# Opening block merged into the first products' block, transfers in order of use, zero products at the opening

## The chip, the cores and the metric

The kernel runs on one core of one Trainium2 chip. The metric is the device time in microseconds, as the median of several runs. The profile and the trace are of one execution on the chip; their times are microseconds from the span's start.

## The reference, cut to what matters

Two transformer-like layers over T = 512 tokens of width 1024. The change touches only the start of the first one: a root-mean-square norm and the first matrix product.

```python
h = rmsnorm(x, norm_mix[i])
u = h @ w_in[i]
u_rwkv = u[..., :RWKV_COLS]
u_da = u[..., RWKV_COLS:RWKV_COLS + DA_COLS]
```

`rmsnorm` divides each token by the root of its mean square and multiplies by the gain `norm_mix`. Since the divisor belongs to a token, the kernel applies it behind the product.

## The kernel before

Everything is kept transposed, channels on the 128 partitions and the 512 tokens along the row; x is 8 tiles (index k) of 128x512. A **job** is one output tile: a weight tile of 128x1024 (8 blocks of 128x128) times the 8 tiles of h. For precision each operand is cut into a high half (`w_hi`, `h_hi`, rounded to fp32r) and a low half (`w_lo`, `h_lo`), so a job is 8 times the three matmuls of lines 367 to 369, 24 in all, of 512 columns each.

The program is a row of blocks with a barrier between them. In the first, the **opening block** (line 2873), SyncE issues the loads (`params`, weight tiles 0 and 1, x in four transfers of two tiles each, `consts`, weight tiles 2 and 3, `w_lora`), and VectorE derives four small constants from `params` (lines 2888 to 2894). The second is `gemm_block` (line 306) with the stages `DaIn` (12 jobs) and `Shift` (15 jobs).

`gemm_block` writes out each engine's order by hand. SyncE streams weight tiles into four raw slots; a tile waits until the low half of the tile four before it is made. ScalarE makes `w_hi` (line 390) and VectorE `w_lo` (line 408), into three slots. The function `due` says how early: before the stage's own work of job g they take all tiles up to the job's own plus the look-ahead, which is `first_ahead` = 1 for job 0 and `AHEAD` = 2 afterwards, as far as a slot is free. TensorE goes through batches of jobs; `DaIn` puts jobs 0 and 1 in one batch and alternates between them at each k. Ahead of a batch, a loop over its jobs issues the waits for their `w_lo`.

In `DaIn`, at job 0, ScalarE makes for each k `h_hi` (line 755) and the square of x (line 760, into the two-row buffer `norm_sq`), VectorE makes `h_lo` (line 765), and GpSimd adds the squares into `norm_pair` (line 778; six adds). ScalarE then loads a table of functions. Ahead of job 2 TensorE sums the squares over partitions by two products with ones (`NormSum.pe`, lines 785 and 787), and at job 1 in ScalarE's order `NormSum.finish` makes `norm_rstd` by a log (line 792), a table load and an exp (line 797). VectorE's outputs (line 658) of jobs 0, 1 and 2 all stand at job 2 in its order, the first behind a wait for `norm_rstd`. From job 3 on attention work (`DiffAttention`, `beside`) is woven in: rotations on TensorE (line 491), their tables loaded by GpSimd's queue behind the square-sum (lines 456 and 457), and sums on VectorE (lines 589 to 593).

Of the kernel before, what the change touches and what calls it, by code (L numbers as in the profile page):

```python
# [16 lines left out]
F32 = mybir.dt.float32  # L17
# [154 lines left out]
BANKS = 4  # L172

# [97 lines left out]
class Stage:  # L271
# [7 lines left out]

    def before(self, pe, n):  # L280
        pass
# [24 lines left out]
def gemm_block(pr, hi, lo, stages, first_ahead=AHEAD, pe_after=nothing, act_after=nothing, dve_after=nothing, sp_after=nothing,  # L306
               sp_between=nothing, behind=nothing):
# [20 lines left out]
    def due(split, g):  # L328

        if split >= tiles or split > weight(g) - first_tile + (AHEAD if g else first_ahead):  # L330
            return False
        s = pr.split_no[first_tile + split] - 1
        return s < SPLIT_SLOTS or pr.last_job[pr.split_slot[s - SPLIT_SLOTS]] <= first + g

    with nc.Block() as block:
# [10 lines left out]
        def _(pe):  # L346
            for batch in batches:
# [10 lines left out]
                for k in range(kt):  # L358
                    for g in batch:
                        stage, n = order[g]  # L360
                        stage.ready(pe, n, k)
                        job = stage.jobs[n]
                        slot = (pr.split_no[job.weight] - 1) % SPLIT_SLOTS
                        w_hi, w_lo = hi[:, slot, k * P:(k + 1) * P], lo[:, slot, k * P:(k + 1) * P]
                        x_hi, x_lo = job.moving[k]
                        out = bank(g)[:, 0:job.width]
                        nc.tensor.matmul(out, w_hi, x_hi, start=(k == 0), stop=False)  # L367
                        nc.tensor.matmul(out, w_hi, x_lo, start=False, stop=False)  # L368
                        last = nc.tensor.matmul(out, w_lo, x_hi, start=False, stop=(k == kt - 1))  # L369
                        if k == kt - 1:  # L370
                            last.then_inc(pr.job_done, 1)
# [8 lines left out]
        def _(act):  # L380
            split = 0
# [15 lines left out]
        def _(dve):  # L397
            split = 0
# [222 lines left out]
class DaIn(Stage):  # L621
# [54 lines left out]
    def pool(self, pool):  # L676
        self.norm.pool(pool)
# [64 lines left out]
class NormSum:  # L742
# [19 lines left out]
    def dve(self, dve, k):  # L762
        if self.gain is not None:
# [3 lines left out]
                .then_inc(self.pr.sum_lo, 1)  # L767

# [2066 lines left out]
def bass_two_blocks(nc, dram, out):  # L2835

    with ExitStack() as ctx:
# [30 lines left out]
        with ExitStack() as in_scope:  # L2868
            hi = pr.tile("w_hi", [P, SPLIT_SLOTS, 1024], F32R, in_scope)
            lo = pr.tile("w_lo", [P, SPLIT_SLOTS, 1024], F32R, in_scope)  # L2870
            loaded, consts_in, made, lora_in = (pr.sem(k) for k in ("params_in", "consts_in", "derived_made", "lora_in"))
            x_in = [pr.sem(f"x_in{j}") for j in range(KT // 2)]
            with nc.Block() as block:
                @block.sync
                def _(sp):
                    sp.dma_start(params[:, :], dram["params"]).then_inc(loaded, 16)
                    pr.stream(sp, 2)
                    for k in range(0, KT, 2):
                        sp.dma_start(x[:, k:k + 2, :], x_view(dram["x"])[:, k:k + 2, :]).then_inc(x_in[k // 2], 16)
# [4 lines left out]
                @block.vector  # L2884
                def _(dve):
                    dve.wait_ge(loaded, 16)

                    nc.vector.tensor_tensor(derived[:, 0:15], pr.param_cols("mu_prev"), pr.param_cols("mu_next"),
                                            ALU.add).then_inc(made, 1)
                    dve.wait_ge(made, 1)  # L2890
                    nc.vector.tensor_scalar(derived[:, 0:15], derived[:, 0:15], -1.0, 1.0, ALU.mult, ALU.add).then_inc(made, 1)
                    nc.vector.tensor_scalar(derived[:, 15:19], pr.param_cols("k_a"), -1.0, 1.0, ALU.mult, ALU.add)\
# [210 lines left out]
```

## Time and profile before

| | |
|---|---|
| median of 3 runs | 1804.69 us (1802.5 to 1805.23) |
| span of the profiled execution | 1802.6 us; no other time of this execution is given |
| TensorE matmuls | 1718.9 us busy, 95% |
| VectorE | 1050.2 us, 58% |
| ScalarE | 705.3 us, 39% |
| GpSimd | 112.8 us, 6% |
| HBM traffic | 94 GB/s over the span |

Busy shares are averages over the whole span. A matmul's duration contains its drain, so the pace is read from the distance between starts. "Idle before" in a row is the time in which the engine stood, with who released it.

### The profile page before, as it was taken

The page shows a single profiled execution, that of the slowest core. Times are in us where ns is not written, and L with a number is a line of the kernel's source. Part 1 is how long each engine was busy: PE and PEld are TensorE (multiplying, and loading weights), DVE is VectorE, ACT ScalarE, POOL GpSimd, SP SyncE. Part 2 cuts the span into 40 slices and gives each one's busy share as a digit, 9 for nine tenths or more (in the row PEclk, how much of TensorE's full clock was granted, in tenths as well). Part 3 has the DMA queues.
Part 4 walks back from the last instruction along what each step waited for, and adds up shares of the span by engine and source line. Part 5 has one row for each costly group of instructions (what it writes and reads, how often), then busy time and mean ns, then how long its engine had stood idle before and what let it go on. Part 6 is the DMA issues. An engine that isn't in the chain of part 4 may idle for free. (4 is left out here: it accounts for less than half of the span.)

```text
span 1802.6 us, 29740 instructions
## 1 busy us (share of the span) xinstructions
PE 1718.9 (95%) x12674; PEld 1350.5 (75%) x12674; DVE 1050.2 (58%) x1461; ACT 705.3 (39%) x1051; POOL 112.8 (6%) x132
## 2 busy tenths in 40 slices
PE   7999999999999999999999889998898899999997
PEld 5666768888876888888888678874476678888885
DVE  6757586667537657677665763117785544343433
ACT  4344544424236443232314443235664433142322
POOL 2000000000000100001111100003100100000001
PEclk9999999999999999999999999999999999999998
DMA  5212221011044344446562222230001222322321
GB/s 201 67 59 77 93 85 38 32 43 38 20 162 161 117 164 140 170 141 226 192 212 84 73 82 71 82 118 2 1 1 48 82 82 94 105 94 94 105 94 47
DMA packets 49076, 171.16 MB, mean 95 GB/s; under 512 B 5536, under 2 KB 6944, under 8 KB 48176
## 3 DMA queue, kind: packets, MB, share of 16 engines
q1 hardware_dynamic: 39184, 133.00, 21.6%
q0 software_dynamic: 9760, 36.25, 6.0%
q8 instruction: 101, 1.65, 0.4%
q14 instruction: 31, 0.25, 0.0%
HBM read 160.84 MB, written 8.39 MB: 94 GB/s over the span
## 5 line engine op out<-in xcount | busy, mean ns | idle before, releaser
L367 PE MATMUL pair<-h_hi,w_hi 128*128 128x512 f32 x1032 | 417.6, 405 | 33.1 <-DVE w_lo L408 15.5
L369 PE MATMUL pair<-h_hi,w_lo 128*128 128x512 f32 x1032 | 405.6, 393 | 0.0
L368 PE MATMUL pair<-h_lo,w_hi 128*128 128x512 f32 x1032 | 405.5, 393 | 0.0
L408 DVE TENSOR_TENSOR w_lo<-w_raw,w_hi 128x1024 fp32r<-128x1024 f32 (+2 forms) x225 | 265.8, 1183 | 201.2 <-ACT w_hi L390 201.1
L390 ACT CAST w_hi<-w_raw 128x1024 fp32r<-128x1024 f32 (+2 forms) x225 | 221.9, 989 | 225.3 <-PE pair L369 221.2
L367 PEld LDWEIGHTS pair<-h_hi,w_hi 128*128 128x128 f32 x1032 | 196.2, 190 | 92.3 <-DVE w_lo L408 31.6
L368 PEld LDWEIGHTS pair<-h_lo,w_hi 128*128 128x128 f32 x1032 | 196.3, 190 | 42.7 <-issue 3.8
L369 PEld LDWEIGHTS pair<-h_hi,w_lo 128*128 128x128 f32 x1032 | 195.8, 190 | 41.9
L367 PE MATMUL pair<-ff_f_hi,w_hi 128*128 128x512 f32 x512 | 199.7, 390 | 0.6 <-issue 0.6
L369 PE MATMUL pair<-ff_f_hi,w_lo 128*128 128x512 f32 x512 | 199.2, 389 | 0.0
L368 PE MATMUL pair<-ff_f_lo,w_hi 128*128 128x512 f32 x512 | 199.2, 389 | 0.0
L2480 ACT ACTIVATE ff_sq<-ff_relu 128x512 f32<-128x512 f32 x64 | 40.5, 632 | 219.6 <-DVE ff_relu L2509 110.4
L367 PEld LDWEIGHTS pair<-ff_f_hi,w_hi 128*128 128x128 f32 x512 | 96.1, 188 | 20.8 <-issue 1.0
L369 PEld LDWEIGHTS pair<-ff_f_hi,w_lo 128*128 128x128 f32 x512 | 96.1, 188 | 19.9
L368 PEld LDWEIGHTS pair<-ff_f_lo,w_hi 128*128 128x128 f32 x512 | 96.1, 188 | 19.9
L2512 DVE TENSOR_TENSOR ff_f_lo<-ff_sq,ff_f_hi 128x512 fp32r<-128x512 f32 x64 | 44.3, 693 | 86.5 <-ACT ff_f_hi L2484 86.5
L2520 DVE SCALAR_TENSOR_TENSOR x<-pair,mod,x 128x512 f32<-128x512 f32 x32 | 24.0, 751 | 88.9 <-PE pair L369 88.9
L2381 DVE SCALAR_TENSOR_TENSOR mod_acc<-mod_w,silu_c,mod_acc 128x1024 f32<-128x1024 f32 x56 | 71.4, 1279 | 1.2 <-DMA mod_w<-in_w_mod 0.9
L861 PE MATMUL pair<-h_hi,gate_hi 128*128 128x512 f32 x128 | 60.5, 473 | 1.9 <-DVE norm_pair L891 1.9
L760 ACT ACTIVATE norm_sq<-x 128x512 f32<-128x512 f32 x40 | 25.0, 624 | 69.1 <-DVE x L2333 34.1
L863 PE MATMUL pair<-h_hi,w_raw_low 128*128 128x512 f32 x128 | 50.6, 396 | 0.0
L862 PE MATMUL pair<-h_lo,gate_hi 128*128 128x512 f32 x128 | 50.5, 394 | 0.0
(418 smaller groups left out, 2519.5 us busy)
## 6 DMA issues: line engine op xcount, KB each, us to landing
w_raw<-in_w_ff SPq DMA_DIRECT2D x128, 512.0 KB, 3.3
mod_w<-in_w_mod POOLq DMA_DIRECT2D x48, 512.0 KB, 3.6
w_raw<-in_w_in SPq DMA_DIRECT2D x22, 512.0 KB, 3.3
w_raw<-in_w_gate SPq DMA_DIRECT2D x16, 512.0 KB, 3.3
w_raw<-in_w_out SPq DMA_DIRECT2D x16, 512.0 KB, 3.3
w_raw<-in_w_rwkv SPq DMA_DIRECT2D x15, 512.0 KB, 3.2
w_raw<-in_w_da SPq DMA_DIRECT2D x12, 512.0 KB, 3.9
w_raw<-in_w_ple_gate SPq DMA_DIRECT2D x8, 512.0 KB, 3.2
```

Source lines behind the costliest of these rows:

```text
L367: nc.tensor.matmul(out, w_hi, x_hi, start=(k == 0), stop=False)
L368: nc.tensor.matmul(out, w_hi, x_lo, start=False, stop=False)
L369: last = nc.tensor.matmul(out, w_lo, x_hi, start=False, stop=(k == kt - 1))
L390: nc.scalar.copy(hi[:, s % SPLIT_SLOTS, 0:cols], pr.raw[:, w % RAW_SLOTS, 0:cols]).then_inc(pr.hi_made, 1)
L408: nc.vector.tensor_tensor(lo[:, s % SPLIT_SLOTS, 0:cols], pr.raw[:, w % RAW_SLOTS, 0:cols], hi[:, s % SPLIT_SLOTS, 0:cols].bitcast(F32), A ...
L760: nc.scalar.activation(pr.sum_sq[:, k % 2, :], self.x[:, k, :], ACT.Square).then_inc(pr.sum_squared, 1)
L861: nc.tensor.matmul(pr.bank[3], w_hi, x_hi, start=(k == 0), stop=False)
L862: nc.tensor.matmul(pr.bank[3], w_hi, x_lo, start=False, stop=False)
L863: last = nc.tensor.matmul(pr.bank[3], w_lo, x_hi, start=False, stop=(k == KT - 1))
L2381: nc.vector.scalar_tensor_tensor(acc, w, c, acc, ALU.mult, ALU.add).then_inc(self.added, 1)
L2480: nc.scalar.activation(self.sq[:, u % 2, :], self.relu[:, u % 2, :], ACT.Square).then_inc(self.sq_made, 1)
L2512: nc.vector.tensor_tensor(self.f_lo[:, g % 2, j, :], self.sq[:, u % 2, :], self.f_hi[:, g % 2, j, :].bitcast(F32), ALU.subtract)\
```

## The change

The opening block is gone. Its loads, derived constants and a table load stand at the head of the first `gemm_block`, in the queues of their own engines, with no barrier behind them. The loads come in the order tile 0, x 0 to 3, tile 1, x 4 to 7, tile 2, `consts`, tile 3, `w_lora`. The look-ahead is 0 for jobs 0, 1 and 2. The halves of h are made four before tile 1 and four after it; all squares come behind them, four before tile 2 and four after; VectorE adds them instead of GpSimd. In the batch of jobs 0 and 1 TensorE does k = 0 to 3 of job 0, then of job 1, then k = 4 to 7 of both. The square-sum moves into job 2, ahead of its k = 4, and `finish` to job 2 on ScalarE. One table load fewer remains. `shift_pad` is filled with zeros by two memsets, and TensorE multiplies them four times at the very start (fp32, into bank 3, which nobody reads). No result changes.

```diff
@@ -170,6 +170,7 @@
 MOD_PARTS = 6
 MOD_SLOTS = 2
 BANKS = 4
+WARM = 4
 
 
 class Job:
...
@@ -277,6 +278,10 @@
     def batches(self):
         return [[n] for n in range(len(self.jobs))]
 
+    def pieces(self, kt):
+
+        return [1] * kt
+
     def before(self, pe, n):
         pass
...
@@ -327,7 +332,7 @@
 
     def due(split, g):
 
-        if split >= tiles or split > weight(g) - first_tile + (AHEAD if g else first_ahead):
+        if split >= tiles or split > weight(g) - first_tile + (AHEAD if g >= len(first_ahead) else first_ahead[g]):
             return False
         s = pr.split_no[first_tile + split] - 1
...
@@ -344,6 +349,7 @@
 
         @block.tensor
         def _(pe):
+            pe_first(pe)
             for batch in batches:
                 for g in batch:
...
@@ -355,20 +361,21 @@
                         old, m = order[g - BANKS]
                         old.freed(pe, m)
                 kt = TILES[weight(batch[0])][2]
-                for k in range(kt):
-                    for g in batch:
-                        stage, n = order[g]
-                        stage.ready(pe, n, k)
...
+                pieces = order[batch[0]][0].pieces(kt)
+                edges = [sum(pieces[:i]) for i in range(len(pieces) + 1)]
+                for k, g in [(k, g) for i in range(len(pieces)) for g in batch for k in range(edges[i], edges[i + 1])]:
+                    stage, n = order[g]
+                    stage.ready(pe, n, k)
...
             pe_after(pe)
...
@@ -622,33 +631,41 @@
 
 
 
-    def __init__(self, pr, jobs, Q, beside, norm, x_in, consts_in, rstd):
+    SPLIT = {0: (0, 1, 2, 3), 1: (4, 5, 6, 7)}
+    SQUARED = {1: (0, 1, 2, 3), 2: (4, 5, 6, 7)}
+
+    def __init__(self, pr, jobs, Q, beside, norm, x_in, consts_in, rstd, start_loads):
         self.pr, self.jobs, self.Q, self.beside, self.norm, self.x_in, self.consts_in, self.rstd = (
             pr, jobs, Q, beside, norm, x_in, consts_in, rstd)
+        self.start_loads = start_loads
 
     def batches(self):
         return [[0, 1]] + [[n] for n in range(2, len(self.jobs))]
 
-    def before(self, pe, n):
-        if n == 2:
+    def pieces(self, kt):
+        return [4, 4]
+
+    def loads(self, sp):
+        self.start_loads(sp)
+
+    def ready(self, pe, n, k):
+        if n < 2:
+            self.norm.split_ready(pe, k)
+        if n == 2 and k == 4:
             pe.wait_ge(self.consts_in, 16)
             self.norm.pe(pe)
-
-    def ready(self, pe, n, k):
-        if n == 0:
-            self.norm.split_ready(pe, k)
         self.beside.pe(pe, n, k)
 
     def freed(self, pe, n):
         pe.wait_ge(self.beside.s["tile_out"], n + 1)
 
     def act(self, act, n, bank, done):
-        if n == 0:
-            for k in range(KT):
-                act.wait_ge(self.x_in[k // 2], 16)
-                self.norm.act(act, k)
-            self.pr.nc.scalar.preload_act_table(ACT.Ln)
-        if n == 1:
+        for k in self.SPLIT.get(n, ()):
+            act.wait_ge(self.x_in[k // 2], 16)
+            self.norm.act_hi(act, k)
+        for k in self.SQUARED.get(n, ()):
+            self.norm.act_square(act, k)
+        if n == 2:
             self.norm.finish(act, self.rstd)
         self.beside.act(act, n)
...
@@ -659,10 +676,12 @@
             .then_inc(self.beside.s["tile_out"], 1)
 
     def dve(self, dve, n, bank, done):
-        if n == 0:
-            for k in range(KT):
-                dve.wait_ge(self.x_in[k // 2], 16)
-                self.norm.dve(dve, k)
+        for k in self.SPLIT.get(n, ()):
+            dve.wait_ge(self.x_in[k // 2], 16)
+            self.norm.dve(dve, k)
+        for k in self.SQUARED.get(n, ()):
+            if 1 <= k < KT - 1:
+                self.norm.dve_add(dve, k)
         self.beside.dve(dve, n)
         self.beside.dve_late(dve, n)
...
@@ -674,7 +693,6 @@
             self.out(dve, n, bank, done)
 
     def pool(self, pool):
-        self.norm.pool(pool)
         pool.wait_ge(self.pr.sum_done, 1)
         self.beside.load(pool)
...
@@ -750,9 +768,15 @@
         pr.sum_splits += gain is not None
 
     def act(self, act, k):
+        if self.gain is not None:
+            self.act_hi(act, k)
+        self.act_square(act, k)
+
+    def act_hi(self, act, k):
+        self.pr.nc.scalar.activation(self.x_hi[:, k, :], self.x[:, k, :], ACT.Copy, scale=self.gain(k)).then_inc(self.pr.sum_hi, 1)
+
+    def act_square(self, act, k):
         pr, nc, u = self.pr, self.pr.nc, self.use
-        if self.gain is not None:
-            nc.scalar.activation(self.x_hi[:, k, :], self.x[:, k, :], ACT.Copy, scale=self.gain(k)).then_inc(pr.sum_hi, 1)
         if k == 1 and u:
             act.wait_ge(pr.sum_done, u)
         if k or u:
...
@@ -765,6 +789,14 @@
             self.pr.nc.vector.scalar_tensor_tensor(self.x_lo[:, k, :], self.x[:, k, :], self.gain(k),
                                                    self.x_hi[:, k, :].bitcast(F32), ALU.mult, ALU.subtract)\
                 .then_inc(self.pr.sum_lo, 1)
+
+    def dve_add(self, dve, k):
+        pr = self.pr
+        dve.wait_ge(pr.sum_squared, k + 1)
+        if k > 1:
+            dve.wait_ge(pr.sum_added, k - 1)
+        one = pr.sum_sq[:, 0, :] if k == 1 else pr.sum_acc[:, :]
+        pr.nc.vector.tensor_tensor(pr.sum_acc[:, :], one, pr.sum_sq[:, k % 2, :], ALU.add).then_inc(pr.sum_added, 1)
 
     def pool(self, pool):
...
@@ -2868,36 +2900,49 @@
         with ExitStack() as in_scope:
             hi = pr.tile("w_hi", [P, SPLIT_SLOTS, 1024], F32R, in_scope)
             lo = pr.tile("w_lo", [P, SPLIT_SLOTS, 1024], F32R, in_scope)
-            loaded, consts_in, made, lora_in = (pr.sem(k) for k in ("params_in", "consts_in", "derived_made", "lora_in"))
+            pad = pr.tile("shift_pad", [P, 2, T + 2], F32, in_scope)
+            loaded, consts_in, made, lora_in, warm = (pr.sem(k) for k in ("params_in", "consts_in", "derived_made", "lora_in", "warm_zeros"))
             x_in = [pr.sem(f"x_in{j}") for j in range(KT // 2)]
-            with nc.Block() as block:
-                @block.sync
-                def _(sp):
-                    sp.dma_start(params[:, :], dram["params"]).then_inc(loaded, 16)
-                    pr.stream(sp, 2)
-                    for k in range(0, KT, 2):
-                        sp.dma_start(x[:, k:k + 2, :], x_view(dram["x"])[:, k:k + 2, :]).then_inc(x_in[k // 2], 16)
-                    sp.dma_start(consts[:, :], dram["consts"]).then_inc(consts_in, 16)
-                    pr.stream(sp, RAW_SLOTS)
-                    sp.dma_start(w_lora[:, :, :], dram["w_lora"].rearrange("p (a n) -> p a n", a=2)).then_inc(lora_in, 16)
-
...
+            def start_loads(sp):
+                sp.dma_start(params[:, :], dram["params"]).then_inc(loaded, 16)
+                pr.stream(sp, 1)
+                for k in range(0, KT, 2):
+                    if k == 4:
+                        pr.stream(sp, 2)
+                    sp.dma_start(x[:, k:k + 2, :], x_view(dram["x"])[:, k:k + 2, :]).then_inc(x_in[k // 2], 16)
+                pr.stream(sp, 3)
+                sp.dma_start(consts[:, :], dram["consts"]).then_inc(consts_in, 16)
+                pr.stream(sp, RAW_SLOTS)
+                sp.dma_start(w_lora[:, :, :], dram["w_lora"].rearrange("p (a n) -> p a n", a=2)).then_inc(lora_in, 16)
+
+            def derive(dve):
+                for j in range(2):
+                    nc.vector.memset(pad[:, j, :], 0.0).then_inc(warm, 1)
+                dve.wait_ge(loaded, 16)
...
+            def table_first(act):
+                nc.scalar.preload_act_table(ACT.Ln)
+                act.wait_ge(loaded, 16)
+
+            def warm_up(pe):
+
+                pe.wait_ge(warm, 2)
+                for _ in range(WARM):
+                    nc.tensor.matmul(pr.bank[BANKS - 1], pad[:, 0, 0:P], pad[:, 1, 0:T], start=True, stop=True)
+
             norm_mix = NormSum(pr, x, h_hi, h_lo, pr.param("norm_mix"))
             spilled = pr.sem("o_spilled")
             h_parts = split_parts(h_hi, h_lo, KT)
             o_hi, o_lo = pr.tile("o_hi", [P, 4, T], F32R, in_scope), pr.tile("o_lo", [P, 4, T], F32R, in_scope)
-            pad = pr.tile("shift_pad", [P, 2, T + 2], F32, in_scope)
             Q = pr.tile("da_in", [P, 12, T], F32, in_scope)
             u_gate = pr.tile("rwkv_gate", [P, T], F32, in_scope)
...
@@ -2929,9 +2974,9 @@
                 sp.wait_ge(lora_in, 16)
 
             gates = Gates(pr, pr.taken + 12 + R_TILES, h_parts, norm_rstd[:, :], gate_hi, pair[:, 0, :], g_spill)
-            da_in = DaIn(pr, [Job(pr.taken + n, h_parts) for n in range(12)], Q, attention, norm_mix, x_in, consts_in, norm_rstd[:, :])
+            da_in = DaIn(pr, [Job(pr.taken + n, h_parts) for n in range(12)], Q, attention, norm_mix, x_in, consts_in, norm_rstd[:, :], start_loads)
             shift = Shift(pr, [Job(pr.taken + 12 + n, h_parts) for n in range(R_TILES)], lambda n: U[:, n, :] if n < R_TILES - 1 else u_gate[:, :], pad, attention, spill, norm_rstd[:, :], gates, activations)
-            gemm_block(pr, hi, lo, [da_in, shift], first_ahead=1, pe_after=first_gate, act_after=lambda act: gates.high(act, 1),
+            gemm_block(pr, hi, lo, [da_in, shift], first_ahead=(0, 0, 0), pe_first=warm_up, act_first=table_first, dve_first=derive, pe_after=first_gate, act_after=lambda act: gates.high(act, 1),
                        dve_after=lambda dve: gates.low(dve, 1), sp_after=landed, behind=gates.plan)
         G = pr.room(0, 32)("gates", [P, 2 * KT, T])
```

VectorE from the start to the first outputs, before (`w_lo` low half of a weight tile, `h_lo` low half of h, `da_in` an output):

```order
L408 TENSOR_TENSOR w_lo<-w_raw,w_hi 128x1024 x2
L765 SCALAR_TENSOR_TENSOR h_lo<-x,params,h_hi 128x512 x8
L573 TENSOR_TENSOR da_lam<-params 128x1 x2
L408 TENSOR_TENSOR w_lo<-w_raw,w_hi 128x1024 x3
L658 SCALAR_TENSOR_TENSOR da_in<-pair,norm_rstd 128x512 x3
L408 TENSOR_TENSOR w_lo<-w_raw,w_hi 128x1024
```

And with the change, VectorE again:

```order
L417 TENSOR_TENSOR w_lo<-w_raw,w_hi 128x1024 [waits w_hi_made]
L789 SCALAR_TENSOR_TENSOR h_lo<-x,params,h_hi 128x512 [waits sum_hi,x_in0] x2
L789 SCALAR_TENSOR_TENSOR h_lo<-x,params,h_hi 128x512 [waits sum_hi,x_in1] x2
L582 TENSOR_TENSOR da_lam<-params 128x1 x2
L417 TENSOR_TENSOR w_lo<-w_raw,w_hi 128x1024 [waits w_hi_made]
L789 SCALAR_TENSOR_TENSOR h_lo<-x,params,h_hi 128x512 [waits sum_hi,x_in2] x2
L789 SCALAR_TENSOR_TENSOR h_lo<-x,params,h_hi 128x512 [waits sum_hi,x_in3] x2
L799 TENSOR_TENSOR norm_pair<-norm_sq 128x512 [waits sum_sq]
L799 TENSOR_TENSOR norm_pair<-norm_pair,norm_sq 128x512 [waits sum_acc,sum_sq] x2
L417 TENSOR_TENSOR w_lo<-w_raw,w_hi 128x1024 [waits w_hi_made]
L799 TENSOR_TENSOR norm_pair<-norm_pair,norm_sq 128x512 [waits sum_acc,sum_sq] x3
L675 SCALAR_TENSOR_TENSOR da_in<-pair,norm_rstd 128x512 [waits job_done,sum_rstd]
L675 SCALAR_TENSOR_TENSOR da_in<-pair,norm_rstd 128x512 [waits job_done] x2
L417 TENSOR_TENSOR w_lo<-w_raw,w_hi 128x1024 [waits w_hi_made] x3
```

Five low halves stood ahead of the three outputs; now three do, and those of tiles 3, 4 and 5 stand behind them.

TensorE at the head of its order, with the change (`pair` is the PSUM bank written):

```order
L2940 MATMUL pair<-shift_pad 128x512 [waits warm_zeros]
L2940 MATMUL pair<-shift_pad 128x512 x3
L374 MATMUL pair<-h_hi,w_hi 128x512 [waits sum_lo,w_lo_made]
L375 MATMUL pair<-h_lo,w_hi 128x512
L376 MATMUL pair<-h_hi,w_lo 128x512
L374 MATMUL pair<-h_hi,w_hi 128x512 [waits sum_lo]
```

Four products are new; the wait for `w_lo_made` stands at the first product of the batch alone.

## Rows read from the trace of the kernel before

**Rows 1.** The page: busy us, share of the span, instructions, of each engine.

```profile
PE 1718.9 (95%) x12674; PEld 1350.5 (75%) x12674; DVE 1050.2 (58%) x1461; ACT 705.3 (39%) x1051; POOL 112.8 (6%) x132
```

**Rows 2.** Timeline of SyncE, opening: start us, us, engine line, what, count.

```profile
1.18 0.90 SPq L259 DMA_DIRECT2D w_raw<-in_w_da  x2
2.12 2.33 SPq L2879 DMA_DIRECT2D x<-in_x  x4
```

**Rows 3.** DMA issues at 1.2, 2.1 and 4.0 us: KB each, us to landing.

```profile
w_raw<-in_w_da SPq DMA_DIRECT2D x1, 512.0 KB, 3.6
...
x<-in_x SPq DMA_DIRECT2D x1, 512.0 KB, 5.8
...
x<-in_x SPq DMA_DIRECT2D x1, 512.0 KB, 8.0
```

**Rows 4.** Timeline of ScalarE (ACT) and VectorE (DVE), opening.

```profile
6.97 1.28 ACT L390 ACT_TABLE_LOAD   x1 [6.97 <-PEq L2873]
8.26 1.99 ACT L390 CAST w_hi<-w_raw 128x1024 fp32r<-128x1024 f32 x2
...
11.62 1.41 DVE L765 SCALAR_TENSOR_TENSOR h_lo<-x,params,h_hi 128x512 fp32r<-128x512 f32 x2
```

**Rows 5.** Timeline of TensorE (PE), its first product.

```profile
12.51 0.76 PE L367 MATMUL pair<-h_hi,w_hi 128*128 128x512 f32 x1 [12.51 <-DVE h_lo L765]
```

**Rows 6.** Windows over jobs 0 and 1: length, busy us (count) of PE, PEld, DVE, ACT, POOL, PEclk, DMA share, GB/s.

```profile
12.51:18.19 5.68, 5.68 (x13) 4.43 (x14) 4.63 (x4) 4.42 (x9) 4.55 (x4) 1.00 1.00 399
18.19:26.21 8.02, 8.02 (x36) 6.61 (x35) 6.70 (x7) 5.60 (x8) 4.50 (x3) 1.00 0.01 3
```

**Rows 7.** Tile x, first 30 us: count, ns min/median/max, first and last start.

```profile
L755 ACT ACTIVATE h_hi<-x,params x8: 704/708/719, 10.2 to 20.1; 128x512 fp32r<-128x512 f32 x8
L760 ACT ACTIVATE norm_sq<-x x8: 612/624/634, 10.8 to 21.3; 128x512 f32<-128x512 f32 x8
L765 DVE SCALAR_TENSOR_TENSOR h_lo<-x,params,h_hi x8: 744/1609/1778, 11.6 to 21.8; 128x512 fp32r<-128x512 f32 x8
```

**Rows 8.** Timeline from the square-sum to the first outputs, PE, ACT, DVE.

```profile
26.21 1.02 PE L785 MATMUL pair<-norm_pair,consts 128*128 128x512 f32 x2
...
33.38 0.39 PE L367 MATMUL pair<-h_hi,w_hi 128*128 128x512 f32 x1
...
28.13 0.69 ACT L792 ACTIVATE norm_rstd<-pair,consts 128x512 f32<-128x512 f32 x1 [1.30 <-PE pair L787]
...
30.13 0.63 ACT L797 ACTIVATE norm_rstd<-norm_rstd 128x512 f32<-128x512 f32 x1
...
26.87 1.23 DVE L408 TENSOR_TENSOR w_lo<-w_raw,w_hi 128x1024 fp32r<-128x1024 f32 x1 [1.30 <-ACT w_hi L390]
...
32.88 1.88 DVE L658 SCALAR_TENSOR_TENSOR da_in<-pair,norm_rstd 128x512 f32<-128x512 f32 x3
34.72 1.23 DVE L408 TENSOR_TENSOR w_lo<-w_raw,w_hi 128x1024 fp32r<-128x1024 f32 x1
```

**Rows 9.** Single lines or tiles on VectorE: ns min/median/max.

```profile
L723 DVE MEMSET shift_pad<- x2: 59/59/59, 108.8 to 108.9; 128x1 f32 x2
...
L605 DVE TENSOR_SCALAR x<-x,da_small x1: 478/478/478, 53.9 to 53.9; 128x512 f32<-128x512 f32 x1
...
L590 DVE TENSOR_TENSOR da_in<-da_in,norm_sq x8: 680/681/682, 36.7 to 76.1; 128x512 f32<-128x512 f32 x8
```

**Rows 10.** Timeline of TensorE: first work after three of its later rests.

```profile
528.40 3.67 PE L2163 MATMUL pair<-rwkv_in,consts 128*128 128x512 f32 x8 [2.14 <-PEq L216]
...
1378.51 0.80 PE L367 MATMUL pair<-h_hi,w_hi 128*128 128x512 f32 x1 [4.95 <-DVE w_lo L408]
...
1454.71 0.50 PE L367 MATMUL pair<-h_hi,w_hi 128*128 128x512 f32 x1 [2.94 <-DVE w_lo L408]
```

**Rows 11.** Windows behind those rests (columns as in rows 6).

```profile
1378.51:1383.37 4.86, 4.86 (x11) 3.80 (x12) 2.22 (x2) 0.59 (x1) 0.00 (x0) 0.50 0.74 234
1455.27:1458.66 3.39, 3.39 (x9) 2.63 (x8) 1.80 (x2) 2.19 (x3) 0.00 (x0) 0.50 0.49 155
532.50:535.90 3.40, 3.40 (x17) 2.79 (x16) 0.87 (x2) 2.82 (x4) 0.00 (x0) 1.00 1.01 428
```

More of the change, by code:

```diff
@@ L303, in loads, with gemm_block @@
         pass
-def gemm_block(pr, hi, lo, stages, first_ahead=AHEAD, pe_after=nothing, act_after=nothing, dve_after=nothing, sp_after=nothing,
-               sp_between=nothing, behind=nothing):
+def gemm_block(pr, hi, lo, stages, first_ahead=(), pe_after=nothing, act_after=nothing, dve_after=nothing, sp_after=nothing,
+               sp_between=nothing, behind=nothing, pe_first=nothing, act_first=nothing, dve_first=nothing):
     nc = pr.nc
@@ L357, in _ @@
                 kt = TILES[weight(batch[0])][2]
-                for k in range(kt):
-                    for g in batch:
-                        stage, n = order[g]
-                        stage.ready(pe, n, k)
[L362 to L371, printed above, removed]
+                pieces = order[batch[0]][0].pieces(kt)
[3 more added lines that the diff above has]
+                    stage.ready(pe, n, k)
+                    job = stage.jobs[n]
+                    slot = (pr.split_no[job.weight] - 1) % SPLIT_SLOTS
+                    w_hi, w_lo = hi[:, slot, k * P:(k + 1) * P], lo[:, slot, k * P:(k + 1) * P]
+                    x_hi, x_lo = job.moving[k]
+                    out = bank(g)[:, 0:job.width]
+                    nc.tensor.matmul(out, w_hi, x_hi, start=(k == 0), stop=False)
+                    nc.tensor.matmul(out, w_hi, x_lo, start=False, stop=False)
+                    last = nc.tensor.matmul(out, w_lo, x_hi, start=False, stop=(k == kt - 1))
+                    if k == kt - 1:
+                        last.then_inc(pr.job_done, 1)
             pe_after(pe)
@@ L380, in _ @@
         def _(act):
+            act_first(act)
             split = 0
@@ L397, in _ @@
         def _(dve):
+            dve_first(dve)
             split = 0
@@ L2870, in bass_two_blocks @@
             lo = pr.tile("w_lo", [P, SPLIT_SLOTS, 1024], F32R, in_scope)
-            loaded, consts_in, made, lora_in = (pr.sem(k) for k in ("params_in", "consts_in", "derived_made", "lora_in"))
+            pad = pr.tile("shift_pad", [P, 2, T + 2], F32, in_scope)
+            loaded, consts_in, made, lora_in, warm = (pr.sem(k) for k in ("params_in", "consts_in", "derived_made", "lora_in", "warm_zeros"))
             x_in = [pr.sem(f"x_in{j}") for j in range(KT // 2)]
-            with nc.Block() as block:
-                @block.sync
-                def _(sp):
-                    sp.dma_start(params[:, :], dram["params"]).then_inc(loaded, 16)
-                    pr.stream(sp, 2)
-                    for k in range(0, KT, 2):
-                        sp.dma_start(x[:, k:k + 2, :], x_view(dram["x"])[:, k:k + 2, :]).then_inc(x_in[k // 2], 16)
-                    sp.dma_start(consts[:, :], dram["consts"]).then_inc(consts_in, 16)
-                    pr.stream(sp, RAW_SLOTS)
-                    sp.dma_start(w_lora[:, :, :], dram["w_lora"].rearrange("p (a n) -> p a n", a=2)).then_inc(lora_in, 16)
[L2884 to L2892, printed above, removed]
-                        .then_inc(made, 1)
-                    nc.vector.tensor_scalar(derived[:, 19:20], pr.param("subln")(0), 1.0 - LAMBDA_INIT, None, ALU.mult)\
-                        .then_inc(made, 1)
@@ new lines, in derive @@
+            def derive(dve):
+                for j in range(2):
+                    nc.vector.memset(pad[:, j, :], 0.0).then_inc(warm, 1)
+                dve.wait_ge(loaded, 16)
+                nc.vector.tensor_tensor(derived[:, 0:15], pr.param_cols("mu_prev"), pr.param_cols("mu_next"),
+                                        ALU.add).then_inc(made, 1)
+                dve.wait_ge(made, 1)
+                nc.vector.tensor_scalar(derived[:, 0:15], derived[:, 0:15], -1.0, 1.0, ALU.mult, ALU.add).then_inc(made, 1)
+                nc.vector.tensor_scalar(derived[:, 15:19], pr.param_cols("k_a"), -1.0, 1.0, ALU.mult, ALU.add)\
+                    .then_inc(made, 1)
+                nc.vector.tensor_scalar(derived[:, 19:20], pr.param("subln")(0), 1.0 - LAMBDA_INIT, None, ALU.mult)\
+                    .then_inc(made, 1)
```

## Prediction, blind

> **What bounds the kernel now.** The page's busy shares come first: TensorE is busy 95% of 1802.6 us [rows 1]. So a change pays only where TensorE stands idle or runs slowly, and every edit here lies in the first 35 us. I read that stretch in order of time: SyncE's queue and the landings [rows 2, 3], VectorE and ScalarE [rows 4], then TensorE [rows 5].
>
> TensorE's first product starts at 12.51 us, just after the first `h_lo` (11.62 plus 0.74). Ahead of it stands the opening block: ScalarE waits for its end, loads a table at 6.97 and makes two casts (8.26 to 10.3). Weight tile 0 had landed at 1.18 + 3.6 = 4.8 us, so ScalarE comes more than 3 us late.
>
> The second thing is the pace. From 12.51 to 18.19 TensorE makes 13 products of 512 columns, 0.43 us each; after that 36 in 8.02 us, 0.2275 us apart [rows 6]. That is 1.2 columns per ns against 2.25: the clock's two levels, 1.2 and 2.4 GHz. (The clock column says 1.00 in both; its first record is the rise at 18.2. Later in the trace it says 0.50 where the same slow pace stands [rows 11].) A stretch at the low level loses about half its length, so this one 2.8 us.
>
> **Part by part.** *Landings.* The 512 KB transfers land some 1.45 us apart: 4.8, then 2.12 + 5.8 = 7.9 for the third, 4.0 + 8.0 = 12.0 for the sixth; so about 6.3, 9.3 and 10.7 between. The change gives the same six places to tile 0, x0-1, x2-3, tile 1, x4-5, x6-7. I keep the times.
>
> *TensorE's start.* The four-and-four cut lets product 1 begin late, but the wait for both `w_lo` tiles still stands ahead of product 0, since the loop over the batch that issues those waits is not cut. So TensorE starts when tile 1's low half is there. ScalarE: table in by 2.1 us; cast 0 from 4.8 to 5.85 (two casts took 1.99 [rows 4]); four `h_hi` of 0.71, the last pair from 7.9 to 9.2; tile 1 lands at 9.3, its cast ends at 10.4. VectorE: low half 0 to 7.1; four `h_lo` by 10.0, at 0.74 each (the median of 1.61 [rows 7] was beside GpSimd's adds, which are gone); low half 1 from 10.45 to 11.7. TensorE at 11.8 instead of 12.5: **0.7 us gained**, not three.
>
> *Products 0 and 1.* 48 matmuls took 13.7 us (12.51 to 26.21). All at the high level they take 48 x 0.2275 = 10.9 and end at 22.7; with the same low stretch at 25.5. No k comes late: `h_lo` 4 to 7 follow from 11.7 to 14.4, and k = 4 is wanted 24 matmuls in, at 17.2 or later.
>
> *Squares and adds.* Eight squares of 0.62 [rows 7] on ScalarE and six adds on VectorE, at 0.68 by the nearest row, an operation on two SBUF tiles [rows 9]. ScalarE's squares begin at 13.4, the third waits for the add behind `h_lo` 7 (15.1), tile 2's cast and low half go between (low half there at 18.6), and the last add ends near 20.7. Products that run to 22.7 at least hide all of it: cost nothing. Were that cover gone, a late tile 2 would cost TensorE up to 18.6 less the end of product 1. GpSimd's adds leave nothing waiting behind them.
>
> *The square-sum* on TensorE moves from ahead of product 2 into its middle, 12 matmuls or 2.73 us later, at the same price (33.38 - 26.21 = 7.17, less 24 x 0.2275, is 1.7). And here the change **adds a wait**. Before, tile 3's low half began at 26.87, long before product 3 at 33.38 [rows 8]. Now the look-ahead is 0 for products 0 to 2, so on VectorE tile 3's low half is queued behind the first three outputs, which wait for `rstd`. From the sum's first part to the end of the exp it took 26.21 to 30.76, 4.55 us. All at the high level: sum at 22.7 + 2.73 = 25.4, `rstd` at 30.0; tile 3's cast ends beside it at 30.9; three outputs at a pitch of 0.61 (32.88 to 34.72) to 31.85; the low half to 33.1; product 3 at **33.1**. Product 2 ended at about 30.0, so TensorE stands for 3.1 us. Before, product 3 began at 33.38: of the 3.5 us won by the end of product 1 only **0.3** is left. With the low stretch kept, all shifts by 2.8 and product 3 begins at 35.9, **2.5 us later** than before.
>
> Behind that nothing differs: in the first reckoning tiles 4 and 5 are done by 35.3 (before, tile 5's low half was 34.72 to 35.95), and the next output waits for the product, not for VectorE. The shift of product 3 goes to the end.
>
> *The zero products.* An fp32 product is two parts (the sum's show x2 [rows 8]) of 0.43 at the high level, so 0.86, and 1.72 at the low one. They start after two memsets: bound below by a one-column memset, 0.06, above by a scalar operation of the same size, 0.48 [rows 9]; I take 0.48, as it has the size, so a start near 1.8. Low stretches after rests last 4.9 to 5.7 us [rows 6, 11], so the level rises near 7 and the four end at 8 (8.7 if it never rises). They wait for nobody and nobody waits for them. But then TensorE **rests again**, for 3.1 to 3.8 us, until 11.8. What rests do [rows 10, 11]: after 2.14 us the pace stayed (17 in 3.40 us); after 2.94 the clock fell half a microsecond into the work and was low for 3.4 us, 1.7 lost; after 4.95 it was low at once for 4.9, 2.4 lost. The rest behind the zero products and the 3.1 us one before product 3 lie between. The first probably takes back what the zero products bought (1.7 if late, 2.8 if whole); the second may cost 1.7 to 2.4 anew. As bounds: either may cost nothing.
>
> The Trainium skill (TensorE: Matmul & The Clock Gate, section "Why this matters for your kernels") advises warming up with matmuls, and warns that idle gaps between bursts bring the low clock back. By its first half alone the sum would be -0.3 us, by the second at both rests +3 to +5; the trace agrees with the second from 2.94 us of rest on.
>
> **Sum and base.** The profiled execution has no other time than its span of 1802.6; the median of the runs, 1804.69, lies 2.1 above it, and I add the shift to the median. A measurement of this kernel can tell about 0.2%, 3.6 us, from no change.
>
> **Cases.**
> 1. *Forecast: one of the two rests costs the level.* The first alone: +1.4 to +2.5. The second alone: -0.3 + 1.7 to 2.4 = +1.4 to +2.1. Middle **+2.0: 1806.7**. For: rows 11. Chance 0.45.
> 2. *Neither does:* -0.3, 1804.4. For: 2.14 us did nothing. Against: both are half as long again. 0.13.
> 3. *Both do (slower):* +3.1 to +4.9, 1808.7 in the middle. It decides once both rests reach about the 2.94 us of rows 10. 0.26.
> 4. *The wait at tile 3 is short* and the level high from the start: up to -3.8, 1800.9. Against: between the sum and `rstd` lie three steps of ScalarE, one a table load. 0.10.
> 5. *The start does not come forward*, because a landing is late now that x goes ahead of tile 1: +0.7 to +1 on one of these. 0.06.
>
> Cases 1 to 3 span 1804.4 to 1809.6; with 1.4 us of scatter in a median of three and part of case 4 the range is 1801.2 to 1810.0. Slower by over 0.2% is more than half of case 3 and an edge of case 1: 0.22. Faster by over 0.2% is case 4 and a little that I don't see: 0.12. The rest, 0.66, is within 0.2%.
>
> **What would show it.** First product at 11.8 us; products 0 and 1 without a wait; 3 us of idle on TensorE before product 3, released by VectorE's `w_lo`, with product 3 at 33 to 36; starts 0.43 apart somewhere behind 11.8 or behind product 3; `h_lo` at 0.74 throughout. I am wrong if product 3 begins before 32 us, if tile 3's low half is ready before product 2 ends, or if the kernels part behind 40 us.

## The result and the profile after

The changed kernel takes 1808.37 us (median of 16 runs, 1806.24 to 1809.42), the kernel before 1803.83 (16 runs, 1801.77 to 1805.23): ratio 1.0023, 95% interval 1.0016 to 1.0031. That is 4.5 us more, slower by a little over 0.2%. The profiled execution took 1808.76, its span 1806.8, 4.2 above the span of before.

The page, busy shares, against [rows 1]:

```profile
PE 1726.6 (96%) x12682; PEld 1353.2 (75%) x12682; DVE 1050.2 (58%) x1469; ACT 704.1 (39%) x1050; POOL 103.8 (6%) x126
```

TensorE's eight added instructions are the four zero products. Its busy time grows by 7.7 us, 5.3 of them the zeros.

The changed kernel's timeline of TensorE, against [rows 5, 8]:

```profile
2.01 5.25 PE L2940 MATMUL pair<-shift_pad 128*128 128x512 f32 x8 [2.01 <-DVE shift_pad L2920]
12.24 0.77 PE L374 MATMUL pair<-h_hi,w_hi 128*128 128x512 f32 x1 [4.99 <-DVE w_lo L417]
...
27.45 1.02 PE L817 MATMUL pair<-norm_pair,consts 128*128 128x512 f32 x2
...
35.10 0.50 PE L374 MATMUL pair<-h_hi,w_hi 128*128 128x512 f32 x1 [3.05 <-DVE w_lo L417]
```

Each zero product, with fp32 operands, shows as two parts here, hence x8 for four. The bracket at a row's end is the rest ahead of it and who ended it. Both rests of the prediction are there, 4.99 us behind the zeros and 3.05 ahead of product 3, and both were ended by VectorE's `w_lo`. Its own timeline at the second one, against [rows 8]:

```profile
17.79 1.22 DVE L417 TENSOR_TENSOR w_lo<-w_raw,w_hi 128x1024 fp32r<-128x1024 f32 x1
18.93 2.27 DVE L799 TENSOR_TENSOR norm_pair<-norm_pair,norm_sq 128x512 f32<-128x512 f32 x3
32.03 1.89 DVE L675 SCALAR_TENSOR_TENSOR da_in<-pair,norm_rstd 128x512 f32<-128x512 f32 x3 [10.82 <-ACT norm_rstd L829]
33.84 3.48 DVE L417 TENSOR_TENSOR w_lo<-w_raw,w_hi 128x1024 fp32r<-128x1024 f32 x3
```

VectorE stands idle for 10.8 us, waiting for `norm_rstd`, with tile 3's low half queued behind the outputs. Before, that low half began at 26.87.

Windows of the changed kernel (columns as in [rows 6]): a low stretch in product 0, the rest of it up to the square-sum, a low stretch in product 3, what follows.

```profile
12.24:15.40 3.16, 3.16 (x8) 2.51 (x9) 3.01 (x5) 2.66 (x5) 0.00 (x0) 0.50 1.04 413
15.40:27.45 12.05, 12.05 (x55) 9.93 (x53) 4.80 (x7) 4.41 (x7) 0.00 (x0) 1.00 0.38 143
35.88:39.29 3.41, 3.41 (x8) 2.08 (x7) 1.44 (x2) 0.17 (x1) 0.00 (x0) 0.50 0.83 263
39.29:42.70 3.41, 3.41 (x15) 2.47 (x14) 3.01 (x5) 0.00 (x0) 0.00 (x0) 1.00 0.55 203
```

The granted clock is 0.50 in both low stretches. The account, as the distance to before: product 0 starts 0.3 us earlier; the 48 matmuls of products 0 and 1 are done 1.5 earlier (product 2 begins at 24.72, the square-sum of before at 26.21), since this low stretch is 3.2 us long and not 5.7; product 3 starts **1.7 later** (35.10 against 33.38); the low stretch in it makes **3.5 later** (VectorE's output of product 3 at 44.46 against 40.99). It is still 3.5 at the first product with `w_lora`, before:

```profile
225.46 1.09 PE L1002 MATMUL pair<-rwkv_in,w_lora 64*128 64x512 f32 x3 [0.51 <-PEq L335]
```

and with the change, with three later rests:

```profile
228.97 1.56 PE L1034 MATMUL pair<-rwkv_in,w_lora 64*128 64x512 f32 x6 [0.51 <-PEq L340]
...
533.10 5.37 PE L2195 MATMUL pair<-rwkv_in,consts 128*128 128x512 f32 x8 [2.15 <-PEq L217]
...
1383.51 0.79 PE L374 MATMUL pair<-h_hi,w_hi 128*128 128x512 f32 x1 [4.95 <-DVE w_lo L417]
...
1458.94 0.56 PE L374 MATMUL pair<-h_hi,w_hi 128*128 128x512 f32 x1 [2.94 <-DVE w_lo L417]
```

The remaining 0.7 of 4.2 is a balance. Against [rows 10] the distance is 4.7 us at the second row, 5.0 at the third and 4.2 at the last. The first 1.2 of it come between 229 and 528, where the granted clock is 1.00 in both executions; their cause was not found. Then the clock counts: after a rest of 2.15 us eight parts take 5.37 us, where after 2.14 us in [rows 10] they took 3.67, and by 560 the distance is 5.4. At later rests, which meet the clock at another moment, 1.2 of that come back.

All this is one execution. A second profiled one of the same kernel (run 11 below) took 1806.70. It has both low stretches too:

```profile
12.18:16.64 4.46, 4.46 (x11) 3.49 (x12) 3.63 (x6) 3.70 (x7) 0.00 (x0) 0.50 1.03 408
35.72:37.14 1.42, 1.42 (x6) 1.20 (x7) 1.42 (x2) 0.00 (x0) 0.00 (x0) 1.00 0.42 55
37.21:40.62 3.41, 3.41 (x8) 1.73 (x6) 1.72 (x3) 0.17 (x1) 0.00 (x0) 0.51 0.88 303
```

Its product 3 starts at 35.72, the first `w_lora` product at 229.65, 4.2 us later than before, and yet its span is only 2.0 longer: it has no low stretch behind its rest at 533, and more comes back behind 1060. So the wait and both low stretches come again, but the end of one execution differs by 2 us from that of another for reasons that lie far behind the edit.

### The profile page after: what moved, and what is told of

The parts are those of the page before. It is cut to its first block and busy times, and to the rows that moved or that the text cites. A ratio compares the mean times of both kernels' runs of the same rounds, so it can differ in the third digit from the quotient of the medians.

```text
span 1806.8 us, 29747 instructions
## 1 busy us (share of the span) xinstructions
PE 1726.6 (96%) x12682; PEld 1353.2 (75%) x12682; DVE 1050.2 (58%) x1469; ACT 704.1 (39%) x1050; POOL 103.8 (6%) x126
```

## The experiments

Two theories. **A**: the loss is the wait of product 3 for tile 3's low half, with the low clock that this rest brings; what the earlier opening could give is held back by the batch's wait for both weight tiles. **B**: the loss lies in what was moved (the adds on VectorE, the later squares) or in the zero products. Each was timed side by side with the kernel before.

**1. Look-ahead 1 at product 2**, the changed kernel otherwise.

```diff
-            gemm_block(pr, hi, lo, [da_in, shift], first_ahead=(0, 0, 0), pe_first=warm_up,
+            gemm_block(pr, hi, lo, [da_in, shift], first_ahead=(0, 0, 1), pe_first=warm_up,
```

> The changed kernel with look-ahead 1 instead of 0 at product 2, so that tile 3's halves are made before the first three outputs. Theory A (the loss is the wait of product 3 for tile 3's low half, and the low clock behind that rest): the 3.05 us idle before product 3 is gone, product 3 begins at 32.0 instead of 35.1, no low stretch behind it; the rotations' products then wait for their tables (they landed near 35.3), so some 2 us of that come back there. Total 3 to 3.5 us below the changed kernel, 1805.0, ratio to before 1.0006. Theory B (the loss is the moved adds and squares, or the rest behind the zero products): nothing changes beyond 0.5 us, 1808.

Measured: 1804.37 us, ratio 0.9999 (0.9991 to 1.0008). The wait at product 3 is gone; its only rest now stands further in, at the rotations, and is ended by a transfer:

```profile
35.87 0.38 PE L494 MATMUL pair<-da_lam,consts 128*128 128x2 f32 x2 [0.57 <-DMA da_rot<-in_rot_da]
```

One number, which moves one weight half ahead in the order of VectorE, gives back 4 of the 4.5 us. In this profile product 0 started later than in the changed kernel's (13.11 against 12.24) and the low stretch behind it was longer (5.35 us against 3.16), so the gain came in spite of a slower opening. From the square-sum (29.33) to the first `w_lora` product (226.71) it took 197.4 us, against 201.5 in the changed kernel (27.45 to 228.97): 4.1 less.

```profile
13.11:18.46 5.35, 5.35 (x13) 4.19 (x14) 4.40 (x7) 4.57 (x8) 0.00 (x0) 0.50 0.97 389
```

A stands.

**2. The wait put into the kernel before**: look-ahead 0 at products 1 and 2.

```diff
-        if split >= tiles or split > weight(g) - first_tile + (AHEAD if g else first_ahead):
+        if split >= tiles or split > weight(g) - first_tile + (AHEAD if g > 2 or first_ahead > 1 else (1, 0, 0)[g]):
```

> The kernel before with look-ahead 0 at products 1 and 2 and nothing else: the suspected wait put into the old kernel alone. Theory A: on VectorE tile 3's low half stands behind output 2, which waits for the end of product 2 (33.5): product 3 begins at 35.5 instead of 33.4, TensorE rests 2 us before it, and the clock may or may not fall (1.7 us more). Total +2.1 to +3.8 us, ratio 1.0012 to 1.0021. Theory B: no change, since the squares, adds and opening are those of before.

Measured: 1812.15 us, ratio 1.0050 (1.0036 to 1.0064), 8 us and twice the upper end of what I had expected. TensorE's timeline:

```profile
32.15 0.79 PE L367 MATMUL pair<-h_hi,w_hi 128*128 128x512 f32 x1 [4.91 <-DVE w_lo L408]
...
41.63 0.50 PE L367 MATMUL pair<-h_hi,w_hi 128*128 128x512 f32 x1 [1.92 <-DVE w_lo L408]
```

The second rest is the one I had reckoned (1.92 us). The first, of 4.91, I had not: in the old order ScalarE makes `norm_rstd` at job 1, so without look-ahead tile 2's cast stands behind it too. Three casts follow the exp at once, at 29.81:

```profile
29.27 0.63 ACT L797 ACTIVATE norm_rstd<-norm_rstd 128x512 f32<-128x512 f32 x1
29.81 2.92 ACT L390 CAST w_hi<-w_raw 128x1024 fp32r<-128x1024 f32 x3
```

And the clock was at 0.50 behind both rests (windows):

```profile
32.15:36.09 3.94, 3.94 (x9) 3.13 (x10) 1.14 (x2) 0.58 (x1) 0.00 (x0) 0.50 0.42 133
42.92:46.33 3.41, 3.41 (x8) 1.77 (x7) 1.52 (x2) 0.17 (x1) 0.00 (x0) 0.50 0.81 257
```

So the mechanism is shown in both kernels. The old order pays more because look-ahead 0 gives it two such rests, not one.

**3. No zero products**, the changed kernel otherwise (`WARM = 0`).

> The changed kernel without the four zero products (the two memsets and the wait stay). Theory A: the zero products buy little, because the clock falls again in the rest behind them: the low stretch at the start is 3.4 to 5.7 us long instead of 3.4, so 0 to +1.2 us against the changed kernel, 1808.4 to 1809.6. Rival (the first half of the rule alone, the zero products keep the clock high): +2.8 us, 1811.

Measured: 1808.08 us, ratio 1.0023 (1.0014 to 1.0032), the changed kernel's own. Where they stand, the four zero products neither cost nor give anything that the medians show. The traces are less tidy: this execution ran at the low pace from 12.49 to 18.18, and its square-sum began at 28.85, 1.4 us later than in the changed kernel's profile and 0.8 later than in its second one (28.06); but behind its 3.05 us of rest ahead of product 3 no low stretch followed:

```profile
36.51:39.92 3.41, 3.41 (x13) 2.22 (x13) 2.77 (x3) 0.17 (x1) 0.00 (x0) 1.00 0.61 183
```

**4. Each product waits for its own tile**, the changed kernel otherwise.

```diff
-                    if g == 0 or w not in [weight(f) for f in range(g)]:
-                        pe.wait_ge(pr.lo_made, pr.split_no[w])
...
+                    if k == 0 and weight(g) not in [weight(f) for f in range(g)]:
+                        pe.wait_ge(pr.lo_made, pr.split_no[weight(g)])
```

> The changed kernel with each product's wait for its weight tile moved to its own first k, instead of both ahead of the batch. Theory A: TensorE starts at 8.8 (h_lo 0 is there at 8.7) instead of 12.2, 1.5 us behind the zero products, so at the high level; it rests some 0.8 us before product 1's first k (tile 1's low half, 12.1); products 0 and 1 end near 20.4 instead of 24.7, and product 3, still waiting for tile 3's low half, begins near 30.9 instead of 35.1. So 4.2 us below the changed kernel, 1804.2, ratio 1.0002. Rival (the start is bound by h, not by the batch's wait): product 0 starts at 12 as now and nothing changes.

Measured: 1803.25 us, ratio 0.9997 (0.9988 to 1.0006).

```profile
8.24 0.47 PE L374 MATMUL pair<-h_hi,w_hi 128*128 128x512 f32 x1 [0.17 <-DVE h_lo L789]
...
12.28 0.50 PE L374 MATMUL pair<-h_hi,w_hi 128*128 128x512 f32 x1 [0.34 <-DVE w_lo L417]
...
30.96 0.79 PE L374 MATMUL pair<-h_hi,w_hi 128*128 128x512 f32 x1 [3.05 <-DVE w_lo L417]
```

The start is 4.0 us earlier, product 1 begins at 12.28 instead of 16.54, and product 3 at 30.96, as forecast; its 3.05 us of rest is still whole, since all of that chain hangs on the square-sum. Both held-back gains are thus found: by the medians this one is worth 5.1 us and that of experiment 1 is worth 4.0.

**5. Both repairs.**

> Both repairs of the changed kernel together: each product waits for its own weight tile, and the look-ahead is 1 at product 2. Theory A: TensorE starts at 8.2 as with the first repair alone, products 0 and 1 end near 20.4 and product 3 begins without a rest near 27.7 instead of 31.0, so no low stretch behind it. The rotations then stand waiting for their matrix, which is loaded behind the square-sum (issued near 25.4, landed near 31): about 2 us of rest in product 3. The rotations at 31.1 against 34.9 before: 3.8 us below before, 1800.3, ratio 0.9979. Rival (GpSimd's adds or something later in the program carries the loss): no better than the first repair alone, 1803.3.

Measured: 1800.24 us, ratio 0.9981 (0.9972 to 0.9990), 8.1 us below the changed kernel, so the two gains nearly add up. The rotations wait for their matrix, though less than I said:

```profile
30.00 0.38 PE L494 MATMUL pair<-da_lam,consts 128*128 128x2 f32 x2 [0.55 <-DMA da_rot<-in_rot_da]
```

**6. Both repairs, and the rotation matrix loaded at once.**

```diff
+        pool.dma_start(self.rot[:, :], dram["rot_da"]).then_inc(self.s["table_in"], 16)
+        wait()
         pool.dma_start(self.table[:, :, :], dram["rope_da"].rearrange("p (a t) -> p a t", a=2)).then_inc(self.s["table_in"], 16)
-        pool.dma_start(self.rot[:, :], dram["rot_da"]).then_inc(self.s["table_in"], 16)
```

> Both repairs, and the rotation matrix loaded at once instead of behind the square-sum; the rope table stays behind it, since it takes the place of the squares. Theory A: the table is issued near 25.3 and lands 4.3 us later, near 29.6; the rotations are then wanted at 29.1, so the rest in product 3 shrinks to 0.5 us. 1.5 us below the two repairs alone, 1798.8, ratio 0.9971. If the matrix's early transfer delays tile 0, up to 0.3 us of it is lost.

Measured: **1799.01 us**, ratio 0.9976 (0.9967 to 0.9985), 4.3 us below the kernel before beside it (1803.26), and 9.4 below the changed kernel's median. Of these 1.2 us lie between this kernel and the one of experiment 5, whose interval overlaps this one's. TensorE's rests near the start are now 0.90, 0.38 and

```profile
29.51 0.38 PE L495 MATMUL pair<-da_lam,consts 128*128 128x2 f32 x2 [0.31 <-DMA norm_sq<-in_rope_da]
```

**7. The same without zero products.**

> The same without the four zero products. Theory A: here they matter, because the work follows them after 0.2 us instead of 5: without them the first products run at the low level, product 0's first 12 take 5.1 us instead of 2.8 (to 13.4 instead of 12.3, where tile 1 holds TensorE anyway), and the low stretch may go on until 15. So +1.1 to +2.5 us against the run with them, 1800 to 1801.3. If zero products are worthless in general, no difference.

Measured: 1800.09 us, ratio 0.9985 (0.9976 to 0.9994), 1.1 us above the run with them; the intervals overlap. The windows of the first 12 matmuls say what happens, with zeros and without:

```profile
8.52:12.19 3.67, 3.29 (x12) 2.02 (x12) 3.35 (x7) 3.37 (x5) 0.00 (x0) 1.00 1.05 410
```

```profile
8.12:12.38 4.26, 4.26 (x10) 3.39 (x11) 3.86 (x7) 3.87 (x6) 0.00 (x0) 1.00 1.04 401
```

12 matmuls in 3.67 us, waits included, against 10 in 4.26. (In the second the clock column has no record before the rise at 12.38; the pace of 0.43 is the low level.) Most of that difference falls into the wait for tile 1: the square-sum begins at 23.23 with zeros and at 23.83 without, and further on even this is gone. The first `w_lora` product stands at the same time in both traces, with zeros and without:

```profile
220.37 1.99 PE L1034 MATMUL pair<-rwkv_in,w_lora 64*128 64x512 f32 x8 [0.51 <-PEq L340]
```

```profile
220.37 1.99 PE L1034 MATMUL pair<-rwkv_in,w_lora 64*128 64x512 f32 x8 [0.51 <-PEq L340]
```

The profiled execution without zeros (1801.90 us against 1799.20) lost its 2.7 us further on, the first 1.2 of them by 300 us, after a low stretch behind a rest at 251 us which the other lacks. That the zero products gave 1.1 us here is therefore not shown.

**8. The square-sum back ahead of product 2**, the changed kernel otherwise.

> The changed kernel with the square-sum back ahead of product 2, look-ahead and the rest as changed. Theory A: rstd comes 2.7 us earlier, so the first two outputs are out of the way; product 3 waits for the end of product 2, then output 2 and the low half of tile 3: 2.0 us of rest instead of 3.05, product 3 1.1 us earlier; the clock may hold, which gives 1.7 more. 1.1 to 2.8 us below the changed kernel, 1805.6 to 1807.3. Rival (the wait has nothing to do with rstd): no change.

Measured: 1806.04 us, ratio 1.0016 (1.0008 to 1.0025), 2.3 us below the changed kernel, 1.8 when each is taken against the kernel before beside it. The rest ahead of product 3 is as reckoned, and this time no low stretch follows:

```profile
34.38 0.50 PE L374 MATMUL pair<-h_hi,w_hi 128*128 128x512 f32 x1 [1.91 <-DVE w_lo L417]
```

With the sum early, output 2 (32.51, at the end of product 2) and not `norm_rstd` is what tile 3's low half waits for.

**9 and 12. The adds back on GpSimd**, the changed kernel otherwise, and **11**, the changed kernel again beside the second of them.

```diff
-        for k in self.SQUARED.get(n, ()):
-            if 1 <= k < KT - 1:
-                self.norm.dve_add(dve, k)
...
     def pool(self, pool):
+        self.norm.pool(pool)
```

> The changed kernel with the six adds of the squares back on GpSimd; squares, look-ahead and opening as changed. Theory A: the adds hide in either place: on GpSimd they take some 1.5 us each instead of 0.69, and the last still ends before the square-sum is wanted at 27.4; product 3 waits as before. Within 0.5 us of the changed kernel, 1808.4. Rival (the move of the adds to VectorE carries the loss): 1803 to 1805.

> The changed kernel with the adds on GpSimd, a second time. Theory A: ratio to before 1.002, as the changed kernel beside it. Rival: 1.0013 again, with the changed kernel at 1.0023.

> The changed kernel itself, side by side with the next run on one chip. It is here because the run with GpSimd's adds came out at 1.0013 where theory A said 1.0023. If that was scatter of the clock behind the two rests, both kernels give the same ratio within 0.0006 here; if the adds on VectorE cost something, this one is slower by about 0.001 again.

Measured: 1806.63 us, ratio 1.0013 (1.0004 to 1.0022); the second time 1807.32, 1.0018 (1.0009 to 1.0027), beside the changed kernel at 1808.51, 1.0023 (1.0014 to 1.0032). The first came out 1.8 us lower than I had said, the second 1.2 lower than its neighbour, 0.0005 in the ratio and inside both intervals. The trace gives the adds no direct part: the rest ahead of product 3 is as long as it was,

```profile
34.98 0.50 PE L374 MATMUL pair<-h_hi,w_hi 128*128 128x512 f32 x1 [3.04 <-DVE w_lo L417]
```

but in this execution no low stretch followed, nor in that of run 12 (window of the first matmuls behind it, clock 1.00):

```profile
34.98:36.63 1.65, 1.65 (x9) 1.37 (x9) 1.65 (x2) 0.00 (x0) 0.00 (x0) 1.00 0.42 62
```

Theory B would have needed 1803 to 1805 and is refuted as the main cause. A smaller part is likely: the 22 runs with the adds on GpSimd lie 2.8 us above the kernel before beside them on average, the 27 runs of the changed kernel 4.1. The difference, 1.3 us, has a standard error of 0.4 if the runs are independent. In the profiled executions it is the low stretch in product 3, which both of the changed kernel have and both with the adds on GpSimd have not. But the adds' place does not decide that alone: in experiment 3 they stand on VectorE, and the clock stayed high.

**10. Nine zero products**, which reach to 11.9.

> The changed kernel with nine zero products instead of four, so that they reach to within 1 us of the first product (12.2) and TensorE has no long rest behind them. Theory A: the clock is high from the first product on; products 0 and 1 end 1.7 to 3.4 us earlier than in the changed kernel (its low stretch there is 3.4 us in one profile, 6.8 in that of the first experiment), and all behind follows, the rest before product 3 included: 1805 to 1806.7. Rival (zeros do not raise the clock, or the rest behind them costs nothing): no change, 1808.4.

Measured: 1806.25 us, ratio 1.0014 (1.0005 to 1.0022), 2.1 us below the changed kernel: the rest behind the zeros was what the opening paid for. The first `w_lora` product, at 227.04, is 1.9 us earlier as well.

```profile
2.00 9.94 PE L2940 MATMUL pair<-shift_pad 128*128 128x512 f32 x18 [2.00 <-DVE shift_pad L2920]
...
25.57 1.02 PE L817 MATMUL pair<-norm_pair,consts 128*128 128x512 f32 x2
...
33.22 0.79 PE L374 MATMUL pair<-h_hi,w_hi 128*128 128x512 f32 x1 [3.04 <-DVE w_lo L417]
```

The square-sum begins 1.9 us earlier than in the changed kernel, product 3 too. Product 0 follows the zeros without a rest, at the high clock. The rest ahead of product 3 is as long as it was.

## Why the prediction was right, and where not

The forecast was 1806.7 us within 1801.2 to 1810.0, most likely no difference beyond 0.2%; 1808.4 came, slower by 0.23% (0.16 to 0.31). That is the size of case 3, which had 0.26 of the chances; slower by over 0.2% had 0.22. As a shift, +2.0 us was forecast and +4.5 came. That the times are only 1.7 apart is luck: the base, a median of three, lay 0.9 above the 1803.83 of sixteen runs. The wait and its place were right; the sizes of what follows were not all.

- **The start.** Forecast 11.8, came 12.24. The step that was off is "I keep the times" of the landings. In the changed kernel, tile 0 was issued at 1.20, the first x pair at 1.67 and tile 1 at 2.65. In this order, from issue to landing:

```profile
w_raw<-in_w_da SPq DMA_DIRECT2D x1, 512.0 KB, 4.0
...
x<-in_x SPq DMA_DIRECT2D x1, 512.0 KB, 5.5
...
w_raw<-in_w_da SPq DMA_DIRECT2D x1, 512.0 KB, 7.2
```

  That is landings at 5.2, 7.1 and 9.8 instead of 4.8, 6.3 and 9.3. The wait for both tiles ahead of product 0, which the diff left where it was, was the right reading; experiment 4 moved it and TensorE started at 8.24.
- **`h_lo` at 0.74.** Median 0.745 over the eight. Right; the sum made of it is 0.3 us short (four from 11.7 end at 14.7, not 14.4), which is hidden as well. The squares and adds ended near 21.2 (20.7 forecast), hidden.
- **The added wait at tile 3.** Forecast 3.1 us of rest with product 3 between 33.1 and 35.9; came 3.05 and 35.10. Experiment 1 takes it away, 2 puts it into the old kernel, 8 shortens it by the amount reckoned.
- **The zero products.** Forecast: bought and taken back. Experiments 3 (nothing lost without them) and 10 (2.1 us gained when they reach the first product) show it; experiment 7 does not show more. They ended at 7.3, not 8: the level had risen at 5.2, not near 7, so they ran short, and the rest behind them was 5 us rather than 3.1 to 3.8. The forecast took 4.9 to 5.7 us for a low stretch and left out the 3.4 us that stand in [rows 11] too.
- **The clock: the step that was off most** is the choice of case 1, "one of the two rests costs the level". In both profiled executions of the changed kernel both did: a low stretch of 3.2 us in product 0 and of 3.4 in product 3, in the second execution of 4.5 and 3.4. The price of the second, 1.7 to 2.4, was right (1.8: from 1.7 us late to 3.5). The rule of the Trainium skill (TensorE: Matmul & The Clock Gate, "Why this matters for your kernels") that gaps between bursts bring the low clock back would have given +3 to +5 at both rests. The traces agree with it at 3.05 and 4.99 us here, not always: of seven executions with 3.04 or 3.05 us of rest ahead of product 3 a low stretch followed in four (the two of the changed kernel, experiments 4 and 10) and none in three (experiments 3, 9 and 12).
- **"The shift of product 3 goes to the end."** This was off, and "the kernels part behind 40 us" was one of the prediction's own signs of being wrong. The distance is 3.5 us at 229, 5.4 at 560 and 4.2 at the end, in the second execution 4.2 at 229 and 2.0 at the end. That 4.5 on the median and 4.2 in the span agree is thus in part the choice of the execution.

The 16 times of the changed kernel fall into two groups, 1806.24 to 1806.91 (7 runs) and 1808.30 to 1809.42 (9 runs), with nothing between. It is tempting to give one group a low stretch in product 3 and the other none, but the record speaks against it: the 1806.70 of run 11 had that stretch, and three of that run's eleven times lie between the groups (1807.35, 1807.62, 1807.89). What sets the time of one execution apart from another's is open.

What else stays open: by what path the adds' place is worth about 1 us, where the 1.2 us between 229 and 528 come from, and whether the last 0.31 us of waiting in product 3 would go if the rope table had a place of its own instead of that of the squares; this was not tried.

## What to carry to other kernels

When work is pulled forward, follow what is queued **behind** each wait on an in-order engine: here an opening that came forward was paid for by a weight half that a look-ahead of 0 had put behind three outputs and their norm. A cut of a loop brings nothing as long as a wait for all of its parts stands ahead of it. And zero products help only if real work follows soon: here rests of 3.8 to 5.0 us behind them were followed by a low stretch in all six executions that had one, rests of up to 0.9 us in none, and between these nothing was tried. So set their number by where they end in the trace, not by a count. Last, when a gain of 1 us is at stake, compare the traces at a landmark just behind the edit as well as the medians: both then tell whether the gain was made where you think.

## What was unexpected of the hardware

- A rest of about 2 us can cost the clock or not, by the moment: eight parts took 3.67 us after 2.14 us of rest before, 5.37 after 2.15 in the changed kernel. Likewise a 3.04 us rest ahead of product 3 was followed by no low stretch in experiment 9 and a 3.05 us one by 3.4 us of it in the changed kernel. A small shift at the start thus moves the whole by 1 to 2 us at places where nothing was edited.
- The landings of the same queue scatter from one execution to the next. In the changed kernel's profile the last opening load was issued at 7.07 instead of 6.09 and the first x pair landed 0.8 us later than what held its place before (7.1 against 6.3). But this is not the order: in ten executions with x ahead of tile 1 that pair landed at 6.1 to 6.5 in eight and at 7.0 to 7.1 in two, the last load was issued at 5.64 to 7.07, and tile 1, on which the first product waits, landed at 9.4 to 10.7.
